# A two-layer hybrid encoder step: the first expert's turned input made by PE from the normalised rows and a seat matrix, its gate split ahead, and the output projection as three rounded products

## The reference, cut to what matters

```python
for l in range(DEPTH):                                   # 2 layers; 272 prompt rows and 128 sample rows
    q, k, v, u = split_projection(h, w_in[l])
    a = prompt_attention(...)                            # 4 heads, two softmax maps each
    p = pool_mixer(...)                                  # 4 channel groups
    h = merge_and_residual(h, a, p, w_out[l], ...)       # layer_norm(ALPHA*h + [a, p] @ w_out), w_out 1024 x 1024
    h = layer_norm(ALPHA * h + moe_ffn(h, ...))          # 16 experts, 2 for each token

def moe_ffn(h, ...):
    probs = softmax(xf @ router_w)
    sel = (probs + router_b).reshape(-1, 4, 4)           # best group of four, then the best two in it
    ...
    for e in range(16):
        hid = silu(xf @ w_gate[e]) * (xf @ w_up[e])      # w_gate, w_up 1024 x 512
        y = y + combine[:, e:e + 1] * (hid @ w_down[e])  # w_down 512 x 1024
```

## Time and profile before

| | |
|---|---|
| median of three runs | 1097.58 us (1094.93 to 1101.83) |
| profiled execution, its own time | 1093.33 us |
| its span | 1091.5 us |
| PE, PE weight loads busy | 87%, 69% |
| DVE, ACT, POOL busy | 76%, 58%, 21% |
| mean granted clock of TensorE | 0.93 of full speed |
| expert stages (from the first `up` product) | layer 0 from 230.9 us, layer 1 from 756.9 us |

### The profile page before, as it was taken

One profiled execution on the slowest core, in us unless ns is written; L12 is line 12 of the kernel. 1 busy time (PEld: TensorE's weight loads), 2 busy tenths in 40 slices (PEclk: granted clock), 3 DMA queues, 4 the chain that ended last, 5 costly groups with the idle time before them and its releaser, 6 DMA issues. The chain is left out here.

```text
span 1091.5 us, 14427 instructions
## 1 busy us (share of the span) xinstructions
PE 953.1 (87%) x4778; PEld 752.7 (69%) x4778; DVE 829.1 (76%) x1206; ACT 637.8 (58%) x908; POOL 227.2 (21%) x251
## 2 busy tenths in 40 slices
PE   3999998779999999999239999976999999999950
PEld 3989654457888888888139896545788888888840
DVE  8866547649989898988396664475899898989836
ACT  4344320248888888887454443113788888888832
POOL 4223311013111111100071233111211111111005
PEclk8999999869999999999759999995999999999985
DMA  9425720538999999996470257234799999999614
GB/s 349 158 100 201 270 96 29 192 119 295 360 375 358 366 360 361 376 367 259 177 236 18 100 198 266 102 105 161 263 366 368 364 370 371 354 363 361 240 50 184
DMA packets 117402, 273.05 MB, mean 250 GB/s; under 512 B 9126, under 2 KB 11422, under 8 KB 117326
## 3 DMA queue, kind: packets, MB, share of 16 engines
q1 hardware_dynamic: 97408, 231.75, 59.0%
q10 hardware_dynamic: 9822, 24.48, 6.5%
q0 software_dynamic: 10112, 16.08, 4.1%
HBM read 267.56 MB, written 25.92 MB: 269 GB/s over the span
## 5 line engine op out<-in xcount | busy, mean ns | idle before, releaser
L1165 DVE TENSOR_TENSOR w_lo<-ring,w_hi 128x1024 fp32r<-128x1024 f32 x256 | 303.3, 1236 | 36.6 <-ACT w_hi L1540 34.0
L1540 ACT ACTIVATE w_hi<-ring 128x1024 fp32r<-128x1024 f32 x256 | 260.8, 1060 | 43.5 <-PE PS L841 27.0
L806 PE MATMUL PS<-w_hi,x_hi 128*128 128x512 f32 x512 | 165.7, 405 | 8.9 <-DVE x_lo L1155 6.9
L811 PE MATMUL PS<-w_lo,x_hi 128*128 128x512 f32 x512 | 163.8, 401 | 0.6 <-DVE w_lo L1165 0.4
L806 PE MATMUL PS<-w_hi,x_lo 128*128 128x512 f32 x512 | 162.2, 398 | 0.0
L1172 DVE TENSOR_TENSOR w_lo<-ring,w_hi 128x1024 fp32r<-128x1024 f32 x128 | 155.4, 1220 | 9.0 <-ACT w_hi L1553 7.0
L1553 ACT ACTIVATE w_hi<-ring 128x1024 fp32r<-128x1024 f32 x128 | 134.8, 1058 | 28.6 <-PE PS L811 28.6
L806 PEld LDWEIGHTS PS<-w_hi,x_hi 128*128 128x128 f32 x512 | 95.3, 191 | 31.1 <-ACT w_hi L1540 5.2
L811 PEld LDWEIGHTS PS<-w_lo,x_hi 128*128 128x128 f32 x512 | 97.3, 191 | 24.8 <-DVE w_lo L1165 2.4
L806 PEld LDWEIGHTS PS<-w_hi,x_lo 128*128 128x128 f32 x512 | 97.9, 191 | 23.2
L1811 POOL DMA_INDIRECT M<-xs,idx x32 | 52.5, 1641 | 287.6 <-PE PS L788 267.2
(11 more groups left out here) (202 smaller groups left out, 1489.5 us busy)
## 6 DMA issues: line engine op xcount, KB each, us to landing
ring<-in_w_gate SPq DMA_DIRECT2D x32, 2048.0 KB, 14.6
ring<-in_w_down SPq DMA_DIRECT2D x32, 2048.0 KB, 15.0
ring<-in_w_up SPq DMA_DIRECT2D x32, 2048.0 KB, 15.4
ring<-in_w_in SPq DMA_DIRECT2D x8, 2048.0 KB, 15.0
ring<-in_w_out SPq DMA_DIRECT2D x4, 2048.0 KB, 7.8
M<-in_cache_k ACTq DMA_DIRECT2D x8, 512.0 KB, 3.4
M<-in_cache_v ACTq DMA_DIRECT2D x8, 512.0 KB, 5.3
M<-ys ACTq DMA_DIRECT2D x4, 1024.0 KB, 6.3
```

Source lines behind the costliest of these rows:

```text
L806: pe.matmul(PS[:, n, :], x[:, c:c + P], w_hi[j][:, k * 512:(k + 1) * 512], start=(j == 0 and k == 0 and x is x_hi[par]), stop=False)
L811: mm = pe.matmul(PS[:, n, :], x_hi[par][:, c:c + P], lo[:, k * 512:(k + 1) * 512], start=False, stop=(j == 3 and k == 1))
L1165: dve.tensor_tensor(lo, w, w_hi[j][:, :].bitcast(F32), ALU.subtract).then_inc(up_lo, 1)
L1540: act.activation(w_hi[j][:, :], quarter(3 * par + n, j)[0], ACT.Copy).then_inc(up_hi, 1)
```

## The change

**Output projection.** `out_part` now multiplies rounded parts in three products. The weights are split in quarters in units 8 to 12: ACT copies to `wo_hi` (in slots 0 and 5), DVE subtracts in place. The operand is split in eight pieces (`XO`): ACT copies to `XOhi` (over `FT`) right after the iteration that made it, POOL subtracts in place (`xo_rest`), between its other work.

**First expert.** DVE makes in `seat` a matrix `seat0`: row token, column place, one where the token goes to expert 0. PE multiplies the tile's normalised rows by it (`first_x`, eight float32 products of 128 columns for each tile) and so adds up expert 0's turned input in banks 2 and 3. POOL no longer gathers for expert 0. The first three quarters of its `w_gate` are split ahead of that input on ACT and DVE.

**Order.** For a tile after the first, DVE does `turned_h` right after the gain, then the shift, then `seat` and `share` of the tile before, then `choose`. `index`, `count_rounds` and the last `share` move behind the first expert's input. The loads of expert 0 all wait for the output projection, and `w_down` of expert 1 waits for the gather of expert 1.

```diff
+        WO_ORDER = (2, 3, 0, 1)
+        WO_AT = {8: [(0, 2)], 9: [(0, 3)], 10: [(0, 0), (0, 1)], 11: [(1, 2), (1, 3)], 12: [(1, 0), (1, 1)]}
+        XO = {"pools": (slice(4, 7), slice(0, NTOK)), "heads01": (slice(0, 2), slice(NMETA, NTOK)),
+              "head2": (slice(2, 3), slice(NMETA, NTOK)), "pool3": (slice(7, 8), slice(0, NTOK)),
+              "frames0": (slice(3, 4), slice(TC[0], TC[0] + P)), "frames1": (slice(3, 4), slice(TC[1], TC[1] + P)),
+              "decode": (slice(3, 4), slice(DEC, NTOK)), "meta": (slice(0, 4), slice(0, NMETA))}
...
@@ SP, round_
                 if first_round:
-                    sp.wait_ge(*d[0])
-                    load(0, expert(t["w_gate"], l, 0))
-                    load_down(l, 0, 5, E0, (proj_ps, 16 * (l + 1)))
                     load_up(l, 1, 3, E0 + 1, [d[3], (proj_ps, 16 * (l + 1))])
-                    sp.wait_ge(*projected)
-                    load(1, expert(t["w_up"], l, 0))
+                    load_up(l, 0, 0, E0, [projected] * 2)
+                    load_down(l, 0, 5, E0, projected)
+                    sp.wait_ge(xg_in[1], 16 * (PAIRS * rb + 1))
                     load_down(l, 1, 2, E0 + 1, projected)
...
@@ PE, out_part
+                    hi, lo = XOhi[:, k, c], OTlo[:, k, c] if k < HEADS else D4lo[:, k - HEADS, c]
+                    for half in halves:
+                        out = PS[0:TN[j], 6 * (n % 2) + half, :]
+                        w, low = (a[:, k % 2, :] for a in wo(half, k // 2)[1:])
+                        pe.matmul(out, hi, w, start=(first and k == ks[0]), stop=False)
+                        pe.matmul(out, hi, low, start=False, stop=False)
+                        mm = pe.matmul(out, lo, w, start=False, stop=(last and k == ks[-1]))
@@ PE, attention
                     if j == 12:
-                        for s in OUT_SLOT:
-                            chunk(s, dense_use(s, l, rb) + 1)
                         pe.wait_ge(proj_sb, 16 * (l + 1))
-                        pe.wait_ge(task_act, emptied(l, TASK[l]["pm", 2])[1])
-                        out_part(l, 0, (4, 5, 6), first=True)
+                        pe.wait_ge(xo_lo, xo_count(l, "pools"))
+                        pe.wait_ge(wo_lo_done, wo_count(l, 0, 3))
+                        out_part(l, 0, (4, 5, 6), halves=(0,), first=True)
                     if j == 13:
-                        pe.wait_ge(mix_done, BASE[l] + 7)
-                        out_part(l, 0, (0, 1, 2))
+                        pe.wait_ge(xo_lo, xo_count(l, "heads01"))
+                        pe.wait_ge(wo_lo_done, wo_count(l, 0, 1))
+                        out_part(l, 0, (0, 1), halves=(0,))
+                        pe.wait_ge(wo_lo_done, wo_count(l, 1, 3))
+                        out_part(l, 0, (4, 5, 6), halves=(1,), first=True)
...
-                pe.wait_ge(task_act, emptied(l, TASK[l]["pm", 3])[1])
-                out_part(l, 0, (7,))
-                pe.wait_ge(mix_done, BASE[l] + 10)
+                pe.wait_ge(wo_lo_done, wo_count(l, 1, 1))
+                out_part(l, 0, (0, 1), halves=(1,))
+                pe.wait_ge(xo_lo, xo_count(l, "pool3"))
+                out_part(l, 0, (2, 7))
+                pe.wait_ge(xo_lo, xo_count(l, "frames0"))
                 out_part(l, 0, (3,), last=True)
...
+            def first_x(l, n):
+                tiles = order(LN1[l])
+                j = tiles[n]
+                pe.wait_ge(h_done, ln_count(LN1[l], n))
+                pe.wait_ge(seat0_done, 4 * l + n + 1)
+                for k in range(KT):
+                    mm = pe.matmul(PS[:, 2 + k // 4, k % 4 * P:(k % 4 + 1) * P], H[0:TN[j], j, k * P:(k + 1) * P],
+                                   seat0[0:TN[j], j, :], start=(n == 0 and k % 4 == 0), stop=(n + 1 == len(tiles)),
+                                   skip_group_check=True)
+                return mm
@@ PE, route
+                for n in range(last - 1):
+                    first_x(l, n)
                 rank(l, last - 1)
                 keys_turned(l, (0, 1))
                 turn_z(LN1[l], last)
-                for n in range(last):
-                    pe.wait_ge(hot_done, 4 * l + n + 1)
-                    index_part(l, n, 5)
                 keys_turned(l, (2, 3))
                 logits(l, last)
+                first_x(l, last - 1)
+                pe.wait_ge(hot_done, 4 * l + last)
+                for n in range(last):
+                    index_part(l, n, 5)
                 rank(l, last)
+                first_x(l, last).then_inc(xt_ps, 1)
+                pe.wait_ge(hot_done, 4 * l + last + 1)
+                index_part(l, last, 5).then_inc(idx_ps, 1)
                 pe.wait_ge(k_kept, HEADS * (l + 1))
                 totals(l)
-                pe.wait_ge(hot_done, 4 * l + last + 1)
-                index_part(l, last, 5).then_inc(idx_ps, 1)
...
@@ DVE, seat
+                dve.tensor_scalar(seat0[p, j, :], CT[p, C_IOTA:C_IOTA + P], rank[:, 0:1], mask[p, j, 0:1],
+                                  ALU.is_equal, ALU.mult).then_inc(seat0_done, 1)
@@ DVE, first round of the experts
+                split_up(0, 0, 0, range(3))
                 turned(0, 0)
+                if seated:
+                    index(rb, 0, 5)
@@ DVE, units: each iteration j, ahead of front(l, j)
+                    for half, part in WO_AT.get(j, ()):
+                        wo_split(l, half, part)
@@ DVE, tiles
-                    ln_h_gain(q, n)
-                    if n + 1 < len(tiles):
-                        ln_h_shift(q, n)
+                    if n >= 1:
+                        ln_h_gain(q, n)
+                    turned_h(q, n)
+                    if n == 0:
+                        ln_h_gain(q, n)
+                    ln_h_shift(q, n)
                     if n >= 1:
                         seat(l, n - 1)
-                    turned_h(q, n)
-                    if n + 1 == len(tiles):
-                        ln_h_shift(q, n)
+                        share(l, n - 1)
                     choose(l, n)
-                    if n + 1 < len(tiles):
-                        share(l, n)
                 seat(l, len(tiles) - 1)
-                index(rb, 0, 5)
-                count_rounds(l)
-                share(l, len(tiles) - 1)
@@ ACT, units: behind the projection's evictions in iteration j: wo_split; at the end of 10 to 14: xo_split
+                    if j == 10:
+                        xo_split(l, "pools", ("pm", 2))
+                    elif j == 11:
+                        xo_split(l, "heads01", ("o", 5))
...
@@ ACT, first round of the experts
+                split_up(0, 0, 0, range(3))
+                if seated:
+                    act.wait_ge(k_out, 48 * (l + 1))
                 turned(0, 0)
@@ POOL
+            def xo_rest(l, what):
+                x, hi, lo = xo(what)
+                pool.wait_ge(xo_hi, xo_count(l, what))
+                pool.tensor_tensor(lo, x, hi.bitcast(F32), ALU.subtract).then_inc(xo_lo, 1)
...
+                    if g == 3:
+                        xo_rest(l, "pools")
                     rms_power(l, 3 * g - 1)
+                    if g == 3:
+                        xo_rest(l, "heads01")
                     rms_power(l, 3 * g)
...
```

More of the change, by code:

```diff
@@ L1192, in pair @@
                     split_up(i, 0, 1, range(4))
+                    if first and seated:
+                        count_rounds(l)
+                        share(l, len(order(LN1[l])) - 1)
                     if not first:
@@ L1513, in mixed, with wo_split, xo_split, moe_round @@
                 last.then_inc(task_act, 1)
[L1514 to L1517 removed]
+            def wo_split(l, rb, half, quarter):
+                s = OUT_SLOT[half]
+                w, hi, _ = wo(half, quarter)
+                if quarter == WO_ORDER[0]:
+                    act.wait_ge(landed[s], 16 * (dense_use(s, l, rb) + 2))
+                    act.wait_ge(proj_ps, 16 * (l + half) if half else 16 * l + 1 + max(POS[c] for c in range(4)))
+                act.activation(hi, w, ACT.Copy).then_inc(wo_hi_done, 1)
+            def xo_split(l, what, task):
+                x, hi, _ = xo(what)
+                act.wait_ge(task_act, emptied(l, TASK[l][task])[1])
+                act.activation(hi, x, ACT.Copy).then_inc(xo_hi, 1)
+            def moe_round(l, rb, r, seated):
                 E0 = 16 * (rb + r)
@@ L1642, in _ @@
                             proj(l, m)
+                    for half, part in WO_AT.get(j, ()):
+                        wo_split(l, rb, half, part)
                     if 3 <= j:
```

136 lines of the change are left out of this document (93 added, 43 removed).

## The result

The changed kernel has a median of 1083.1 us (four runs, 1082.86 to 1083.27), beside 1099.7 for the kernel before in the same session (four runs, 1094.93 to 1102.8): a ratio of 0.988, 95% interval 0.985 to 0.990. 1084.3 was forecast. The profiled execution took 1082.86 us (1080.0 forecast) with a span of 1081.1, 10.4 less than before.

A forecast was written before the change was run, and what follows sets the result against it. PE bounds the experts, so gains lie ahead of each first `up`. Attention's ends 2 x 7, tiles -9.2 -5.3, first experts -6.2 -6.6: -13.3 us, from 1093.33 to 1080.0 profiled, 1084.3 median; range 1072 to 1099.

The forecast's parts named there:

- The tiles: Between residuals: 15.0 us each after the second, bound by DVE; first pairs 17.5 and 16.2; in all -9.2 and -5.3.
- T: End of attention in each layer: added splits make the first residual about 7 us later.
- Unit 10's part: Attention's unit 10: two weight splits without cover delay `front`, and with it PE's `av`, by 2.0 us.
- In units 8 and 9 a chunk's products cover one split each: Attention's units 8 and 9: weight splits hide and cost nothing; without that cover, 1.2 us each.
- The other three terms: Attention's end: +1.3 us net in units 11 and 12, +1.5 after the last `av`, +2.0 for the clock.
- The clock term: Attention's end: longer PE waits put 4 us more of PE work at 1.2 instead of 2.4 GHz, +2.0 us.
- R: Last residual to first `up` product: -6.2 us in layer 0, -6.6 in layer 1.
- If that cover goes and the store lands 3 us later, R loses 2: First expert's input: if the keys' stores land 3 us later, ACT's copy waits and 2 us of gain go.
- Expert stages: The experts' products after the first `up`: length unchanged, with PE the bound and loads hidden.
- the splits hide: Rival at attention's end: DVE loses nothing beside POOL and the clock holds; -23 us, 1074; chance 0.2.
- attention's end pays all back: Rival in units 10 to 12: ACT, DVE and POOL take turns instead of overlapping; +13 us, 1110; chance 0.13.
- the first expert isn't earlier: Rival after the last residual: `x_hi` waits for keys' stores, or the clock is low; -4.5 us, 1093; chance 0.17.

The follow-up runs named there:

- run 3: Changed kernel with DVE's order within a tile as in the kernel before (gain, shift, seat, turned_h, choose, share): 1093.5 us.
- run 4: Changed kernel with the output projection multiplying float32 operands again, without its splits on ACT, DVE and POOL: 1080.7 us.
- run 7: Changed kernel with POOL's operand remainders made for only 4 columns of each piece, the third product reading the rounded part instead: 1074.0 us.
- run 11: Changed kernel with three quarters of `w_gate` split after the first expert's input instead of ahead of it: 1084.4 us.
- run 2: Changed kernel with the first expert's rounded input `x_hi` in `FT`'s place instead of the keys' place: 1071.2 us.
- run 10: Changed kernel with `x_hi` in `FT`'s place, the projection's operand split by tile, and unit 10's weight splits moved to units 8 and 9: 1060.8 us.
- run 8: Changed kernel with the float32 output projection, without splits, and `x_hi` in `FT`'s place: 1069.5 us.
- run 6: Changed kernel with expert 0's rows gathered by POOL and turned by PE again, without `seat0` and `first_x`: 1089.2 us.
- run 9: Changed kernel with `x_hi` in `FT`'s place and only the first tile's operand columns split ahead of the first residual: 1065.1 us.
- run 1: Changed kernel with unit 10's two weight splits moved to units 8 and 9, under projection products: 1079.8 us.
- run 5: Changed kernel with unit 10's weight splits moved to units 8 and 9 and `x_hi` in `FT`'s place: 1072.3 us.

## Why the prediction was right, step by step

**The tiles** came out as worked: 15.0 forecast, 15.41, 14.81 and 14.80 measured, bound by DVE; 17.5 forecast for layer 0's first pair, 17.50 measured; 16.2 for layer 1's, 16.98 measured. Three products cost 0.70 us. The reason stands as well: runs 3 and 4 show that order and product each shorten the choice's wait for logits and only both together remove it; in layer 0 each alone gives 3 us where both give 9. The Trainium skill, TensorE: Matmul & The Clock Gate, Back-to-back issue gap, has 216 ns for a lone product of 512 columns; the trace has 233 again (0.70 for three), and where DVE is the bound the difference changes nothing.

**T** was +7.15 and +6.7 against +7. Unit 10's part was +1.9 (122.09 less 119.55, less the 0.66 by which unit 9's `front` was already late) against +2.0. That 0.66 is a step the prediction had at nothing: "In units 8 and 9 a chunk's products cover one split each". The other three terms (1.3 net in units 11 and 12, 1.5 behind the last `av`, 2.0 for the clock) make 4.8, and 4.6 is what is left of 7.15. Run 7 gives all of that to POOL, 5.0 and 4.8 us with what it does to the clock. The clock term was nearer 2.7: the fourteen steps from 137.37 to 143.35, most of them of 0.43 us, take 5.98 where 0.233 each would be 3.26. How much of it a given execution pays is in part luck: run 11 does the same work with nearly the same waits, had six products at 0.43 instead of twelve, and its residual came 1.2 us sooner after unit 11's `front`. So the sum was right within what the executions scatter, with one term left out.

On the rule of the Trainium skill, SBUF — State Buffer, Who interferes with whom: POOL's 1.81 us piece began at 135.50, before DVE's pair at 136.41, and its 2.73 us piece at 126.84, before DVE's at 127.75. DVE came second both times and was stretched by 1.7 and 0.8 us (run 7), less than the whole of either POOL instruction: nearly what was left of it when DVE came, 1.82 and 0.90. The trace agrees with the Trainium skill: the one that starts second waits for the rest of the other. It shows the other order too, which the rows of before did not: POOL's second step of the power (L1921) takes 0.56 us at 113.63, and 1.39 at 130.82, where DVE's pair had begun first.

**R** is where a step failed: "landing 5.0 to 5.6 us later, 19.1, plus the copy: 20.1, level with DVE". The stores landed 8.3 to 10.9 us after issue. `x_hi` started at +22.1 and +21.7 instead of +19.1. The clause for this case, "If that cover goes and the store lands 3 us later, R loses 2", gave the size: 1.9 and 0.8 were lost. Run 2 shows the wait for the stores as the cause. That the stores were slow because of the loads is argued, not tried by itself: before, they were issued with one 2 MB load still on its way, which landed at 219.8, and took 4.3 to 5.7 us; now two were on their way, which landed at 215.8 and 223.8. The step behind it is the loads' own time. The prediction had the third landed 15 us after the last residual; it landed at +22.3 in both layers (in layer 0 issued at 200.71, landed at 223.8). I had counted the loads' effect on the weights only.

**Expert stages** were to be unchanged; layer 1's was 2.2 us longer. Of run 2's 3.0 us there, 2.1 are the pace of the pairs and only 1.1 the first pair, so that at most 1.0 of the 2.2 belongs to the same wait; the rest stays open.

**The number.** That 1084.3 stands beside 1083.1 is in part luck. Span by span the forecast was 13.3 us less and 10.4 came, the profiled execution being 2.9 us above its 1080.0: R lost 2.7 and layer 1's experts 2.2, and the stretch to layer 1's projection gave 1.8 back. The forecast of the median added the 4.25 us by which the profiled execution of the kernel before lay under its median; the changed kernel's runs lie within 0.4 us of one another, with no such distance.

**The rivals.** That the splits hide was wrong for this placement and right for the work: in run 10 T is +0.6 and +0.1. That attention's end pays all back did not occur, and the chain it named (ACT, DVE, POOL in turn) exists, at half the price. That the first expert isn't earlier holds in part by the mechanism it named, the stores behind three loads, at a cost of 1.9 and 0.8 us where it had 4.4 in each layer.

**Where the gain comes from.** The three-product projection by itself is worth nothing as placed (run 4: 1080.7 against 1083.1), and some 8 us once its operand is split by tile and unit 10's splits are moved (run 10 against run 8). By the ratios, undoing the order costs about 9 us (run 3) and undoing the first expert's part about 7 (run 6).

## What to carry to other kernels

Split an operand in the order in which it is consumed, not in the order in which it becomes ready: 1,792 columns of POOL's work moved from the chain into a hole took 5.6 and 5.7 us off the end of attention in the two layers, counted from unit 7's `front`. If a change moves loads, forecast every small store or load beside them with as many loads in flight as there will be, and do not let an input wait for a store only because they share memory. A product made cheaper pays in full only together with the order that lets its consumer use it. And when two executions are compared, start the count where their code begins to differ.

## What the runs showed of the hardware

- A store of 512 KB took 4.4 and 5.6 us in the kernel before, with one load of 2 MB in flight, and 8.3 and 8.9 in the changed kernel, with two; the DMA share was 1.0 in both (410 GB/s over 214.2 to 218 before, and over 211.7 to 217 after).
- A pair of DVE subtractions (128x1024) took 2.36 us alone, 4.05 and 3.12 beside one POOL subtraction each. The difference, 1.69 and 0.76, is nearly what was left of POOL's instruction, 1.82 and 0.90. POOL's small step took 1.39 instead of 0.56 us when it came second.
- The stretch from 136 to 144 had a granted clock of 0.57 in the changed kernel and 1.00 in runs 7, 9 and 10, where POOL's pieces ahead of it were short; runs 1 and 5 had 0.79 and 0.64. With the changed kernel's code in this stretch run 2 had 0.59 and run 11 0.79, the latter after waits of PE of 3.70, 1.30 and 1.53 us against 3.69, 1.71 and 1.53. So shorter waits ahead of it went with a higher clock, but the same code gave both levels in different shares. At the lower level twelve products of the first tile took 0.43 us instead of 0.23.
- In layer 1 R was 21.1 and 21.2 us in runs 2 and 10, where the last tile's logits took 1.93 us, and 23.1 and 24.4 in runs 5 and 9, with identical code there, where they took 3.56 at the lower level.
- With `x_hi` in `FT`'s place instead of the keys', two rounded products of the first expert of each pair took 0.454 us instead of 0.464, at full clock and without waits.
